# A two-layer encoder with a mixture of experts: expert 0's tokens are selected by a product on TensorE, and the routing buffers move

## What is computed

```python
h2 = rms_norm(x, g_norm2[l]) * (1.0 + sc2) + sh2
x = x + gt2 * hier_moe(h2, w_router_group[l], w_router_expert[l], w_exp_gate[l], w_exp_up[l], w_exp_down[l])
...
def hier_moe(h, w_rg, w_re, w_gate, w_up, w_down):
    lg = (xt @ w_rg).astype(F32)
    pg = jax.nn.softmax(lg, axis=-1)
    grp = jnp.argmax(lg, axis=-1)                       # one group of 4
    ...
    top_v, top_i = lax.top_k(le, TOP_K_INNER)           # two of its 8 experts
    gates = p_grp * jax.nn.softmax(top_v, axis=-1)
    ...
        hdn = jax.nn.silu(xe @ w_gate[e_i]) * (xe @ w_up[e_i])
        return hdn @ w_down[e_i]
```

## Time and profile before

| | us |
|---|---|
| three runs: median, lowest, highest | 1788.22, 1786.84, 1789.93 |
| the profiled execution: its own time | 1790.88 |
| the profiled execution: span of the core | 1789.1 |
| PE busy in the span | 1587.5 (89%) |
| DVE, ACT, POOL busy | 716.6, 434.7, 160.1 |
| granted TensorE clock, mean | 0.967 |

### The profile page before, as it was taken

The page is one execution under the profiler, slowest core; times in us unless marked ns, Lnnn a source line. Parts: engine busy times, 40 slices in busy tenths (PEclk is TensorE's granted clock), DMA queues, the critical chain, the costliest instruction groups (busy, mean ns, idle before and its releaser), DMA issues.

```text
span 1789.1 us, 22316 instructions
## 1 busy us (share of the span) xinstructions
PE 1587.5 (89%) x7460; PEld 769.3 (43%) x7460; DVE 716.6 (40%) x1461; ACT 434.7 (24%) x995; POOL 160.1 (9%) x184
## 2 busy tenths in 40 slices
PE   5999999998998998888889999999899989887883
PEld 2455645463333343333345555455433333333331
DVE  1577466672222212122157855743522222222124
ACT  2111467112111111111121016741111112111112
POOL 0000000111111011111000000001110111111010
PEclk9999999989999999999989999999999999999997
DMA  9625532479999999999972365213899999999995
GB/s 360 236 71 189 211 116 95 162 285 367 407 397 403 408 406 399 412 410 414 368 280 94 116 214 197 82 48 109 316 402 399 402 412 403 407 412 401 398 410 199
DMA packets 124293, 528.44 MB, mean 295 GB/s; under 512 B 17184, under 2 KB 23328, under 8 KB 77568
## 3 DMA queue, kind: packets, MB, share of 16 engines
q1 hardware_dynamic: 106704, 491.46, 70.1%
q0 software_dynamic: 12480, 24.51, 4.3%
q10 hardware_dynamic: 4976, 10.55, 1.6%
HBM read 520.96 MB, written 23.86 MB: 305 GB/s over the span
## 4 chain that ended last, share of the span: by engine, by line
PE 65%; DMA 13%; SPq 9%; DVE 5%; ACT 4%; issue 4%; ACTq 0%; DVEq 0%; POOLq 0%
PE ps L1411 24%; PE ps L1050 18%; DMA ring<-in_w_exp_up 7%; PE ps L1263 6%; SPq L870 6%; PE ps L1409 4%; PE ps L1205 2%; SPq L860 2%; PE ps L1219 2%; PE ps L1245 2%; DMA arena<-in_w_exp_up 2%; ACT arena L1688 2%; ACT arena L1702 1%; DMA hT<-in_w_exp_up 1%; DMA ring<-in_w_in 1%
## 5 line engine op out<-in xcount | busy, mean ns | idle before, releaser
L1411 PE MATMUL ps<-ring,arena 128*64 128x512 f32 x1728 | 490.7, 609 | 48.6 <-ACT arena L1702 29.9
L1411 PEld LDWEIGHTS ps<-ring,arena 128*64 128x64 f32 x1728 | 158.2, 140 | 280.8 <-issue 270.6
L1050 PE MATMUL ps<-ring,hT 128*128 128x512 f32 (+1 forms) x768 | 254.8, 487 | 2.9 <-DMA ring<-in_w_in 1.9
L743 DVE TENSOR_TENSOR arena<-ps,arena 64x512 f32<-64x512 f32 (+1 forms) x64 | 44.4, 693 | 458.5 <-ACT arena L1696 380.1
L1696 ACT ACTIVATE arena<-ps 128x512 f32<-128x512 f32 x64 | 38.2, 597 | 756.3 <-PE ps L1411 705.5
L1050 PEld LDWEIGHTS ps<-ring,hT 128*128 128x128 f32 x768 | 144.3, 190 | 102.7 <-issue 91.0
L751 DVE TENSOR_TENSOR arena<-ps,gate 64x512 f32<-64x512 f32 (+1 forms) x64 | 43.7, 683 | 283.2 <-PE ps L1411 263.1
L1015 POOL DMA_INDIRECT yexp_d<-arena,masks x64 | 59.7, 932 | 838.3 <-DVE arena L753 775.0
L1411 PE MATMUL ps<-home,arena 128*64 128x512 f32 x320 | 122.3, 601 | 11.1 <-ACT arena L1702 5.1
L1411 PE MATMUL ps<-work,arena 128*64 128x512 f32 x288 | 111.2, 613 | 9.1 <-ACT arena L1702 5.1
L1411 PE MATMUL ps<-hT,arena 128*64 128x512 f32 x272 | 107.5, 613 | 7.8 <-ACT arena L1702 4.7
(11 more groups left out here) (233 smaller groups left out, 1734.7 us busy)
## 6 DMA issues: line engine op xcount, KB each, us to landing
ring<-in_w_exp_up SPq DMA_DIRECT2D x80, 1024.0 KB
ring<-in_w_exp_down SPq DMA_DIRECT2D x78, 1024.0 KB
ring<-in_w_exp_gate SPq DMA_DIRECT2D x74, 1024.0 KB
ring<-in_w_ada SPq DMA_DIRECT2D x24, 2048.0 KB, 11.0
ring<-in_w_in SPq DMA_DIRECT2D x8, 2048.0 KB, 21.9
home<-in_w_exp_gate SPq DMA_DIRECT2D x16, 1024.0 KB
hT<-in_w_exp_down SPq DMA_DIRECT2D x12, 1024.0 KB
work<-in_w_exp_gate SPq DMA_DIRECT2D x12, 1024.0 KB
```

The source lines that it names most:

```text
L1050: last = pe.matmul(out, lhs(k), rhs(k), start=(k == 0), stop=(k == n - 1))
L1411: last = [pe.matmul(outs[c][HALF * c:HALF * c + HALF, :], lhs(k)[:, 0:HALF], rhs(c, k), start=(k == 0), stop=(k == n - 1), tile_position=( ...
```

## The change

Expert 0's tokens are no longer gathered. TensorE makes them by a product: `pick` (128 tokens x 4 tiles x 128 slots) has, in the row of a token of expert 0, its 1/rms in the column of its slot, and `x` (in SBUF) times `pick`, summed over the four tiles, gives the turned and normalised tokens straight into banks 3 and 4 (`pick_tokens`). The list products move behind and between the two halves of this, and the overflow's list behind expert 0's gate and up products. The routing buffers leave `work` for `wr`, `z`, `rT` and `masks`, and the tenth unit's load waits for other things. Both `mods` stand ahead of the rank products. The gates are computed later on VectorE, and `gfin` is loaded later. Units 10 and 11 are loaded with their first halves together and then their second halves. The core of the diff:

```diff
-        hot = prob[0][:, 0:2 * TT * NE].rearrange("p (k t e) -> p k t e", k=2, t=TT)
-        hots5 = prob[1][:, 0:TT * NE + NE]
+        hot = wr[:, :, :].rearrange("p k e -> p (k e)")[:, 0:2 * TT * NE].rearrange("p (k t e) -> p k t e", k=2, t=TT)
+        hots5 = z[:, 1, 360:360 + TT * NE + NE]
...
-        slot_hot = arena[:, 5120:6144].rearrange("p (n r) -> p n r", r=P)
+        slot_hot = arena[:, 3072:4096].rearrange("p (n r) -> p n r", r=P)
+        pick = arena[:, 0:S].rearrange("p (t r) -> p t r", t=TT)
+        place = z[:, 0, 400:400 + TT]
...
             await_drained(dve, key)
+            link(dve.scalar_tensor_tensor(place, rk[:, :, 0], 1.0, hots[:, :, 0], ALU.add, ALU.mult))
+            link(dve.tensor_scalar(place, place, -1.0, None, ALU.add))
+            dve.wait_ge(xn_out, 16 * TT * (l + 1))
+            for t in range(TT):
+                last = dve.tensor_scalar(pick[:, t, :], C["iota"], place[:, t:t + 1], rstd[:, t:t + 1], ALU.is_equal, ALU.mult)
+            last.then_inc(pick_ready, 1)
...
+            first_tokens()
             slot_lists((l, "lists"), 0, NE).then_inc(gidx_ready, 1)
...
-            expert_tokens(0, 0)
+            rest = route(dve, link, mods_out, l, lambda: expert_tokens(0, 0))
             words = wide_words(dve, l)
-            rest()
             expert_hidden(0, 0, 0)
             expert_tokens(1, 1)
+            rest()
...
                     if b == WORK:
-                        sp.wait_ge(slots_ready, 2 * l + 2)
-                        sp.wait_ge(xg_in[0], 16 * (l * HE + 1))
+                        sp.wait_ge(rin_ready, 2 * l + 1)
+                        await_drained(sp, (l, "out", TT - 1, 1))
                         if ADA_NEXT[l]:
                             await_filled(sp, (l + 1, "mods", 1))
...
-                for m in range(NBUF, 3 * TURN):
+                for h in range(2):
+                    for c in range(2):
+                        if h:
+                            sp.wait_ge(filled[c], expert_bank(l, c) + 1)
+                        else:
+                            sp.wait_ge(gate_up_half, NE * l + 1)
+                        load_half(NBUF + c, NBUF // 3, h)
+                for m in range(NBUF + 2, 3 * TURN):
                     expert_unit(0, m)
...
-                for e in range(2):
-                    gather(e)
+                gather(1)
+                if l == DEPTH - 1:
+                    pool.wait_ge(slots_ready, 2 * l + 2)
+                    for c0, part in gfin:
+                        pool.dma_start(part, view(a["g_final"], c0, [[0, P], [1, part.shape[1]]])).then_inc(gfin_in, 16)
...
-                if ADA_NEXT[l]:
-                    mods(0)
+                for n in range(len(ADA_NEXT[l]) // 2):
+                    mods(n)
...
-                idle_products(3, 1)
...
+                def pick_tokens(half):
+
+                    b = 3 + half
+                    await_bank_free(b, 0)
+                    for i in range(4):
+                        for t in range(TT):
+                            last = pe.matmul(bank_e(b)[:, P * i:P * i + P], x[:, t, 4 * half + i:D:KD], pick[:, t, :],
+                                             start=(t == 0), stop=(t == TT - 1))
+                    last.then_inc(filled[b], 1)
...
                     def arrived(h):
 
+                        pe.wait_ge(drained[3 + h], at(3 + h, e) + 1)
                         for c in range(2):
                             half_arrived(q, n, c, h)
 
                     def body(w):
-                        pe.wait_ge(drained[3], at(3, e) + 1)
-                        pe.wait_ge(drained[4], at(4, e) + 1)
...
+                pe.wait_ge(pick_ready, l + 1)
+                pick_tokens(0)
                 words = wide_words(pe, l)
-                turn_tokens(0, 0)
-                idle_products(1, 1)
...
+                fills(last, key)
+                pick_tokens(1)
...
                 gate_up(0, 0)
+                key = (l, "more_lists")
```

More of the change, by code:

```diff
@@ L717, in rest, with experts_dve @@
                 dve.sem_inc(more_ready, 1)
+                dve.wait_ge(rexp_ready, 2 * (l + 1))
+                link(dve.tensor_reduce(rt[:, pgrp:pgrp + TT], r3(diff), AX_X, ALU.add))
+                link(dve.tensor_scalar(gates[:, 0, :], rt[:, dv:dv + TT], 1.0, None, ALU.add))
+                link(dve.tensor_tensor(gates[:, 0, :], gates[:, 0, :], rt[:, pgrp:pgrp + TT], ALU.mult))
+                link(dve.reciprocal(gates[:, 0, :], gates[:, 0, :]))
+                link(dve.tensor_tensor(gates[:, 1, :], gates[:, 0, :], rt[:, dv:dv + TT], ALU.mult))
+                kept, moved = rt[:, 36:40], rt[:, 44:48]
+                dve.tensor_tensor(kept, found[:, 0], found[:, 1], ALU.is_lt)
+                link(dve.tensor_tensor(moved, found[:, 0], found[:, 1], ALU.is_gt))
+                parts = [rt[:, hotg + TT * i:hotg + TT * i + TT] for i in range(4)]
+                for i in range(2):
+                    dve.tensor_tensor(parts[2 * i], gates[:, i, :], kept, ALU.mult)
+                    last = dve.tensor_tensor(parts[2 * i + 1], gates[:, 1 - i, :], moved, ALU.mult)
+                link(last)
+                for i in range(2):
+                    link(dve.tensor_tensor(gates[:, i, :], parts[2 * i], parts[2 * i + 1], ALU.add))
             return rest
-        def experts_dve(dve, l, rest):
+        def experts_dve(dve, link, mods_out, l):
             def at(b, e):
@@ L986, in _ @@
                         pool.tensor_tensor(xh, xh, tmp[:, n, :], ALU.add).then_inc(mixed, 1)
-                if l == DEPTH - 1:
-                    for n in range(2):
-                        await_drained(pool, (l, "out", TT - 1, n))
-                    for c0, part in gfin:
-                        pool.dma_start(part, view(a["g_final"], c0, [[0, P], [1, part.shape[1]]])).then_inc(gfin_in, 16)
                 pool.wait_ge(xn_out, 16 * TT * (l + 1))
-                for j in range(2):
-                    link(pool.memset(xg[j], 0.0))
+                link(pool.memset(xg[1], 0.0))
                 words = wide_words(pool, l)
@@ L1345, in _ @@
                 fills(pe.matmul(bank(key)[:, 0:n], C["before"], hots5, start=False, stop=True), key)
-                if ADA_NEXT[l]:
-                    mods(1)
-                else:
-                    idle_products(2, 1)
-                key = (l, "list_parts")
-                pe.wait_ge(slots_ready, 2 * l + 1)
-                await_free(pe, key)
-                for r in range(2):
-                    for q in range(4):
-                        last = pe.matmul(bank(key)[NE * q:NE * q + NE, 0:P], slot_val[:, 4 * r + q, 0:NE], slot_hot[:, 4 * r + q, :],
-                                         start=(r == 0), stop=(r == 1), tile_position=(0, NE * q))
-                fills(last, key)
-                key = (l, "lists")
-                await_free(pe, key)
-                fills(pe.matmul(bank(key)[:, 0:NE], list_parts, C["fold32"], start=True, stop=True), key)
-                idle_products(3, 1)
-                key = (l, "more_lists")
-                pe.wait_ge(slots_ready, 2 * l + 2)
-                await_free(pe, key)
-                fills(product(bank(key)[:, NE:P], lambda n: slot_hot[:, n, :], lambda n: slot_val[:, n, NE:P], n=2 * TT), key)
                 def bank_e(b):
@@ L1457, in down @@
                     by_width(pe, words, TURN // 2 * q + n // 2, j, body)
+                pe.wait_ge(pick_ready, l + 1)
+                pick_tokens(0)
                 words = wide_words(pe, l)
-                turn_tokens(0, 0)
-                idle_products(1, 1)
+                key = (l, "list_parts")
+                pe.wait_ge(slots_ready, 2 * l + 1)
+                await_free(pe, key)
+                for r in range(2):
+                    for q in range(4):
+                        last = pe.matmul(bank(key)[NE * q:NE * q + NE, 0:P], slot_val[:, 4 * r + q, 0:NE], slot_hot[:, 4 * r + q, :],
+                                         start=(r == 0), stop=(r == 1), tile_position=(0, NE * q))
+                fills(last, key)
+                pick_tokens(1)
+                key = (l, "lists")
+                await_free(pe, key)
+                fills(pe.matmul(bank(key)[:, 0:NE], list_parts, C["fold32"], start=True, stop=True), key)
                 gate_up(0, 0)
+                key = (l, "more_lists")
+                pe.wait_ge(slots_ready, 2 * l + 2)
+                await_free(pe, key)
+                fills(product(bank(key)[:, NE:P], lambda n: slot_hot[:, n, :], lambda n: slot_val[:, n, NE:P], n=2 * TT), key)
                 turn_tokens(0, 1)
```

36 lines of the change are left out of this document (9 added, 27 removed).

## The result

The change makes the kernel slower: 1805.96 us median (1803.95 to 1809.71, 4 runs) against 1787.81 (1786.84 to 1789.93, 4 runs) of the kernel before on the same chip, ratio 1.0104, 95% interval 1.009 to 1.0118. The forecast was 1785.4 us and its range ended at 1789.5. The profiled execution took 1809.71 us, the longest of the four, and its span is 1807.9.

The account below looks back on a forecast made before the run. Each expert stage was taken to end on its last weight DMA, so idle DMA early costs time. Gains of 2.0 us (layer 0) and 0.8 (layer 1) sum to 2.8: 1788.22 - 2.8 = 1785.4 us, range 1781.0 to 1789.5.

Parts of the forecast that it names:

- the price of a row of the products with `pick`: Expert 0's token products on TensorE: 0.108 us a row of 128 columns, 6.9 us for 32 two-row products at full clock.
- The steps ahead of it: From the `mods` and rank products to `pick`, before expert 0's products: `pick` ready at 394.1 in layer 0, 1266.1 in layer 1.
- The clock rival: The products with `pick` don't raise TensorE's clock: start 5.5 us later than forecast per layer, 8.2 us lost, 1796; 10%.
- The rule set against the forecast: FP32 transpose mode is four times faster, so the 32 products with `pick` would take twice 6.9 us and the sum come out slower.
- The loss of a late start: Clock rival's cost of gate and up starting 5.5 us late: 5.5 - 2.0 us in layer 0, 5.5 - 0.8 in layer 1.
- The gain of an early start: Expert 0's gate and up starting earlier restarts the weight loads earlier: 2.0 us in layer 0, 0.8 in layer 1.
- the step on the restart: Weight queue's restart behind half of gate and up, layer 0: units 10 and 11 land 1.8 to 3.0 us earlier.
- hidden anyway: Rival: places of expert 1 and 2 bind, not the restart; gain 0.4 us a layer, 1787.4; 20%.
- Two costs were put at nothing: Costed at nothing: expert 0's gathers, the gates beside its down products (2 us a layer if uncovered), the buffers' new places.
- The gathers of expert 0: Removing expert 0's token gathers was costed at nothing, since they moved while the DMA queue was dry.
- the gain vector: `gfin`'s loads in layer 1, now at about 1281, share the engines just restarted: 0.5 MB, 1.3 us.

Follow-up runs that it names:

- e1: Changed kernel, but the products with `pick` take 128 neighbouring columns of x instead of every eighth; 1791.98 us, ratio 1.002.
- e11: Changed kernel, stride kept, with `mods_out` ahead of expert 0's hidden row and both gain vector loads early; 1799.71 us, ratio 1.0071.
- e2: Kernel before, with eight products or transposes of each form (contiguous or strided operands) added behind its last expert; 1788.11 us.
- e8: e5 with both of the gain vector's loads issued before layer 1's routing; 1787.49 us, ratio 0.9993.
- e5: e1 with `mods_out` ahead of expert 0's hidden row and the gain vector's first load before the routing; 1789.5 us, ratio 1.0008.
- e4: Kernel before, with only the loads of units 10 and 11 reordered: both first halves, then both second halves; 1786.0 us, ratio 0.9994.
- e10: e4 run once more, beside the kernel before on the same chip; 1788.07 us, ratio 0.999.

## Why the prediction was wrong

**The term that failed is the price of a row of the products with `pick`.** The forecast wrote: "Thirty-two rows of 512 columns took 13.81 us at the full clock, 0.43 each, so a row of 128 columns is 0.108". It scaled the moving columns and left out the load of the stationary ones, 128 columns of x eight values apart. Measured: 0.245 us a row, so 15.7 us for 64 rows rather than 6.9 plus 2.55. The sign of the forecast hung on it. The trace of before held the price, in `mods`, whose stationary operand has 64 such columns, eight values apart. The earlier trace rows has its 32 rows in 3.48 us, 0.109 each, and that alone doesn't give it away, for contiguous columns at the half clock cost as much (0.21 for 128 in e1). The starts do (first at a granted clock of 1.00, then at 0.50):

```profile
L1331 PE MATMUL ps<-cst,arena x7: 258/258/280, 384.0 to 384.8; 128*64 128x1 f32 x7
...
L1331 PE MATMUL ps<-cst,arena x10: 258/258/258, 386.1 to 387.2; 128*64 128x1 f32 x10
```

A row of 64 columns takes 0.8 / 6 = 0.13 us at the full clock and 1.1 / 9 = 0.12 at half of it. It isn't shorter at the full clock, and twice 0.12 is the 0.24 of 128 columns. I used these rows for the time of `mods` and not for their operands.

**The steps ahead of it held.** `pick` was ready 9.7 us behind hT's load (396.20 - 386.52; forecast 394.1 - 384.13, 10.0), the clock rose in the products, `pick` cost 1.13 us and not 0.8, and in layer 1 its wait for the write of `xn2_d` cost nothing. In e1, where the row is cheap, the half clock lost 6.36 - 3.77 = 2.6 us of the first half, as the forecast's 2.55, and gate and up start 20.5 and 20.0 us behind hT's load where 20.5 and 19.0 were forecast.

**The clock rival's time came nearest, by another mechanism.** It had gate and up 5.5 us later than forecast, and said that "a price of a product of 0.43 us gives the same". The product cost 0.49 us, and the start came 5.6 us late in layer 0 of e11 against e1. But the clock was at 1.00 from 402, so that the sizes are alike is luck. The price is of the load: one takes 338 ns at the half clock and 336 at the full one (L1389 in the changed kernel), and 192 where it is contiguous (L1501 in e2). The rule set against the forecast came near the size too, with its estimate of twice the sum's 6.9 us (13.8; measured 15.7), and from a wrong place: it spoke of transposes, and a transpose takes 0.11 us where a contiguous product takes two rows of 0.11 (e2), half and not a quarter.

**The loss of a late start was too small.** The rival took 5.5 - 2.0 = 3.5 and 5.5 - 0.8 = 4.7 us against before; e11, with both side costs off, lost 6.4 and 6.5. Between e8 and e11 a start 5.9 and 6.1 us later ended the stages 6.9 us later, both times: the whole delay and more.

**The gain of an early start was too large.** The 2.8 us never came. With the right price and no side cost (e8), gate and up start 2.1 and 0.6 us sooner than before and the stages end 0.5 and 0.4 us sooner, less than one profile's scatter; the time, 0.9993 (0.998 to 1.0005), can't tell it from none. Against e2, the second profile of the kernel before, gate and up start 1.2 us sooner in layer 0 and as early in layer 1. In layer 0 8.4 MB land 3.0 us sooner, as the step on the restart had it (2.2 against e2), but when 21 MB have landed only 1.5 us of it are left (62.0 against 63.5; 0.7 against e2), and the down products start only 0.5 us sooner. That fits the case called hidden anyway, where the places bind and the gain is 0.4 us a layer; a gain of that size is below what these profiles can tell. In layer 1 the down products start 0.9 us later than before.

**Two costs were put at nothing.** One is `mods_out` behind expert 1's tokens: the forecast named the gates there and not bank 2 (1.6 us at the down products, e5; 3.8 us in the profiled layer 0 with the clock's fall, e11). The clock's fall wasn't seen in e1, which has the same wait (1.00 in its windows from 414 to 418); what decides it is open, since no run varied that alone. The other is layer 1's small transfers. "The gathers of expert 0" were rightly free, and those of experts 1 and 2 weren't named; the gain vector was put at 1.3 us by its bytes, and its second part alone, moved away, brought the profiled stage's end 2.9 us forward (e8 against e5; the four profiles with late loads end 1.5 to 4.4 us behind the six without).

**How the 18 us divide:** stride 14, side costs 6, each give or take 4, and the rest of the change a gain of 1.3 (0.9993) that isn't shown. In the profiled executions: 18.8 us in the stages, less 2.7 us between them and plus 2.8 us ahead of and behind them, 18.8 in all (rounded apart). The 2.7 us are not the change's: between the layers profiled executions took either 367.1 to 367.6 or 369.4 to 369.9 us, and so did two executions of one kernel (e4 and e10, before and e2). Nor, it seems, are the 2.8: most of them lie ahead of hT's load in layer 0, which goes out at 386.52 in the changed kernel, at 382.09 in e11 with the same work before it, and at 384.13 and 383.56 in the two profiles of the kernel before.

**Not tried:** a copy of x with its columns rearranged, from which the products could read side by side. The normalised copy stands where `pick`, xgT and the second experts' rows go, and keeping it would need 4096 more values a partition.

## What to carry to other kernels

Price a product by both operands: look for a row in the trace that loads the stationary operand in the same pattern, and compare starts, not durations. In a stage that ends on the weights, ask of each small transfer whether it runs while their queue is dry; one that is moved behind a restart costs its packets' time there. And a step that is made earlier helps only as far as the next release of a place does (here nothing that could be measured), while one made later was paid in full (6.9 us for 6).

## What was unexpected of the hardware

- Strides of 4 and 8 FP32 values in the stationary operand, and 8 in the moving one, double a row of 128 columns (0.23 against 0.11 us), while stride 2 (0.12) and transposes of stride 8 (0.11) cost nothing more (e2).
- With stride 8 a row of 128 columns takes the same at both levels of the clock, 0.24 us; contiguous it takes 0.21 at 1.2 GHz and 0.11 at 2.4 (e1). So the stride is nearly free at the half clock and doubles the row at the full one.
- A load that copies one row of 256 values to 128 partitions is dear for its bytes. Its 128 KB took GpSimd's queue from 10.7 to 20.7% of the engines in 14 us, 1.4 us (e8, e5), and its landing 7.9 us; the stage ended 2.9 us later.
